# Joints between the six blocks of a two-model transformer kernel: last two output units tile by tile, norm weights at the eviction, constants multiplied meanwhile

## What is computed

```python
h = rmsnorm(x, g[0])
x = x + 0.5 * rmsnorm(swiglu(h, w_gate[0], w_up[0], w_down[0]), g[1])
h = rmsnorm(x, g[2])
x = x + rmsnorm(token_mixer(h, w_in, w_out, ...), g[3])
h = rmsnorm(x, g[4])
x = x + 0.5 * rmsnorm(swiglu(h, w_gate[1], w_up[1], w_down[1]), g[5])
# swiglu: (silu(h @ w_gate) * (h @ w_up)) @ w_down;  256 tokens, width 1024, w_gate and w_up 1024 x 2816
```

## Time and profile before

| what | value |
|---|---|
| median of three runs | 1611.62 us (1608.76 to 1612.12) |
| the profiled execution | 1613.51 us |
| its span in the trace | 1611.7 us |
| PE busy / DVE busy / ACT busy | 92% / 60% / 44% of the span |
| chain that ended last | PE 80%, DVE 8%, ACT 5%, DMA 4% |
| mean granted clock of PE | 0.964 |
| second model begins (last matmul of the first ends) | 514.4 us |

### The profile page before, as it was taken

The page is one execution under the profiler, slowest core; times in us unless marked ns, Lnnn a source line. Parts: engine busy times, 40 slices in busy tenths (PEclk is TensorE's granted clock), DMA queues, the critical chain, the costliest instruction groups (busy, mean ns, idle before and its releaser), DMA issues.

```text
span 1611.7 us, 21802 instructions
## 1 busy us (share of the span) xinstructions
PE 1477.5 (92%) x7995; PEld 1195.7 (74%) x7995; DVE 967.3 (60%) x1508; ACT 709.3 (44%) x1205; POOL 65.1 (4%) x92
## 2 busy tenths in 40 slices
PE   4598999989997999989987999989999899889998
PEld 2476765777853888879866888878888787678886
DVE  1369615344523667676666767776777656576775
ACT  2332215332134444455557444454444555654443
POOL 2000111010001000000000000000000000100000
PEclk9699999999999899999999999989999999999999
DMA  9422138423314565645323565636566443246562
GB/s 321 139 79 79 52 105 282 153 78 114 112 53 148 185 220 171 212 156 183 105 79 118 192 199 183 206 109 223 168 209 206 144 131 110 68 141 229 164 205 74
DMA packets 187807, 246.02 MB, mean 153 GB/s; under 512 B 4224, under 2 KB 168480, under 8 KB 187488
## 3 DMA queue, kind: packets, MB, share of 16 engines
q1 hardware_dynamic: 183872, 229.43, 44.0%
q0 software_dynamic: 3296, 13.64, 2.4%
q10 hardware_dynamic: 576, 2.10, 0.4%
HBM read 244.10 MB, written 1.05 MB: 152 GB/s over the span
## 4 chain that ended last, share of the span: by engine, by line
PE 80%; DVE 8%; ACT 5%; DMA 4%; issue 2%; POOL 1%; SPq 0%; DVEq 0%; ACTq 0%; POOLq 0%
PE bank L1495 30%; PE bank L1919 20%; PE bank L1920 10%; PE bank L1581 4%; DMA weight_ring<-in_w_ada 3%; DVE arena L1220 1%; PE bank L1848 1%; PE bank L1478 1%; PE bank L1899 1%; PE bank L1793 1%; DMA weight_ring<-in_w_ffn_up 1%; DVE weights_low L1226 1%; ACT weights_high L819 1%; PE bank L1516 1%; ACT silu_gate L853 1%
## 5 line engine op out<-in xcount | busy, mean ns | idle before, releaser
L1919 PE MATMUL bank<-input_split,weights_high 128*128 128x512 f32 x1408 | 504.3, 400 | 4.7 <-DVE input_split L1264 4.7
L1226 DVE TENSOR_TENSOR weights_low<-weight_ring,weights_high 128x1024 fp32r<-128x1024 f32 x328 | 396.5, 1224 | 155.6 <-ACT weights_high L819 154.3
L819 ACT ACTIVATE weights_high<-weight_ring 128x1024 fp32r<-128x1024 f32 x328 | 339.5, 1055 | 213.6 <-PE bank L1920 77.7
L1920 PE MATMUL bank<-input_split,weights_low 128*128 128x256 f32 x1408 | 396.8, 282 | 0.0
L1919 PEld LDWEIGHTS bank<-input_split,weights_high 128*128 128x128 f32 x1408 | 266.5, 189 | 71.0 <-issue 6.0
L1920 PEld LDWEIGHTS bank<-input_split,weights_low 128*128 128x128 f32 x1408 | 267.8, 190 | 3.1
L1495 PE MATMUL bank<-weights_high,hidden_high 128*128 128x512 f32 x352 | 138.3, 393 | 0.8 <-DVE hidden_low L1306 0.7
L1495 PE MATMUL bank<-weights_low,hidden_high 128*128 128x512 f32 x352 | 137.9, 392 | 0.0
L1495 PE MATMUL bank<-weights_high,hidden_low 128*128 128x512 f32 x352 | 137.0, 389 | 0.0
L874 ACT ACTIVATE hidden_high<-hidden 128x256 fp32r<-128x256 f32 x88 | 36.8, 418 | 197.9 <-DVE hidden L1302 193.6
L1495 PE MATMUL bank<-input_split,weights_high 128*128 128x256 f32 x512 | 95.7, 288 | 0.7 <-DVE input_split L1264 0.7
(11 more groups left out here) (305 smaller groups left out, 2073.7 us busy)
## 6 DMA issues: line engine op xcount, KB each, us to landing
weight_ring<-in_w_ffn_gate SPq DMA_DIRECT2D x44, 1024.0 KB, 5.9
weight_ring<-in_w_ffn_up SPq DMA_DIRECT2D x44, 1024.0 KB, 5.5
weight_ring<-in_w_ffn_down SPq DMA_DIRECT2D x44, 1024.0 KB, 5.0
weight_ring<-in_w_in SPq DMA_DIRECT2D x42, 1024.0 KB, 5.3
weight_ring<-in_w_ada SPq DMA_DIRECT2D x24, 1024.0 KB, 7.2
weight_ring<-in_w_out SPq DMA_DIRECT2D x16, 1024.0 KB, 4.9
scaled_out<-in_norm_gains POOLq DMA_DIRECT2D x6, 512.0 KB, 3.9
gain_row<-in_norm_gains POOLq DMA_DIRECT2D x6, 512.0 KB, 3.9
```

Of the source, the lines that this page charges most:

```text
L819: A(unit_in(WH, U), unit_source(U), ACT.Copy).then_inc(s_high, 1)
L1226: TTn(unit_in(WL, U), unit_source(U), unit_in(WH, U).bitcast(F32), ALU.subtract).then_inc(s_low, 1)
L1919: mm(b[:, :].rearrange("p (h n) -> p h n", h=2), unit_in(WH, U)[:, k, :], HX[:, k, :, :], start=(k == 0), stop=False, skip_group_check=True)
L1920: last = mm(b[:, 0:T], unit_in(WL, U)[:, k, :], HH[:, k, :], start=False, stop=(k == KD - 1), skip_group_check=True)
```

## The change

- **Output units.** In the last pair of an FFN the second half of the previous down slot is used after both `gate_up`, as unit a+4 (before: a+2). The last two units, both halves of the last down slot, run tile by tile: token tile 0 for both units, then token tile 1. The last two units of a mixer likewise.
- **Tail.** DVE gains and updates token tile 0, then token tile 1.
- **Norm weights.** For the four chunks 0 to 3 (columns 0 to 511) DVE no longer multiplies with `pre_row` (`TS` instead of `STT`); the weight is a per-partition scalar, taken from six added rows of `k_vec2`, and goes in where the transposed chunk is copied out (ACT `scale=`, DVE `STT`). These four chunks are split one by one (128x256), in banks 4 and 5, with waits that keep ACT and DVE in different banks; chunks 4 to 7 in pairs as before. `pre_row` is loaded by half. The transposes of a site now use banks 4, 5, 2, 3.
- **Constants multiplied.** PE starts each `site_norm` with float32 matmuls of the identity with 512 columns of constants into bank 0, four per joint (`WARM`), twelve at site 0. Their result is not used.
- **Splitting ahead.** `EARLY = 2` units of the next site are split before the tail instead of three, so four (`range(EARLY, SPLIT)`) follow after `site_norm`. In a mixer the last two output units are split earlier. The load of the table for the square root moves ahead of the last `hidden_high` of an FFN.

```diff
+EARLY = 2
+WARM = 4
@@ UNITS2
-    UNITS2 += [(m, 0, "c"), (m + 1, 0, "c")] + ([(m - 1, 1, "r")] if q else []) + [(m, 1, "c"), (m + 1, 1, "c"), (m + 2, 0, "r")]
+    back = [(m - 1, 1, "r")] if q else []
+    late = q == FFN_PAIRS - 1
+    UNITS2 += [(m, 0, "c"), (m + 1, 0, "c")] + ([] if late else back) + [(m, 1, "c"), (m + 1, 1, "c")] + (back if late else []) + [(m + 2, 0, "r")]
@@ sync, ffn
-                with sp.Fori(0, FFN_PAIRS - 1) as j:
+                with sp.Fori(0, FFN_PAIRS - 2) as j:
...
+                for q, src in enumerate((g, u, d)):
+                    fill(b0 + 3 * (FFN_PAIRS - 1) + q, src[FFN_PAIRS - 1], 0 if q == 2 else 256)
@@ scalar, site_norm
-                for b in range(4):
-                    act.wait_ge(*at("x_T", "site", i, b))
-                    A(HH[:, 2 * b:2 * b + 2, :], B[b][:, :].rearrange("p (q n) -> p q n", q=2), ACT.Copy).then_inc(*done("input_high", i, b))
+                for c in range(4):
+                    act.wait_ge(*(at("x_T", "site", i, c) if c < 2 else at("input_ready", i, c - 2)))
+                    A(HH[:, c, :], B[4 + c % 2][:, c // 2 * T:(c // 2 + 1) * T], ACT.Copy, scale=vT[:, 2, R_PRE + 8 * i + c:R_PRE + 8 * i + c + 1]).then_inc(*done("input_high", i, c))
+                for c in (4, 6):
...
@@ scalar, ffn, after the loops
+                a, f = a + 5 + 6 * (FFN_PAIRS - 2), f0 + FFN_CHUNKS - 2
+                high(a + 6)
+                silu(0, f + 1, f - 1)
+                hidden_high(0, f + 1, a - 1)
+                for U in range(a + 7, min(len(UNITS2), a + 7 + EARLY)):
+                    high(U)
+                silu(1, f + 2, f)
                 A(stat[:, 60:61], eps[:, 0:1], ACT.Sqrt)
+                hidden_high(1, f + 2, a + 4)
@@ scalar, sites (vector likewise, with low)
-                for unit in range(3, SPLIT):
+                for unit in range(EARLY, SPLIT):
                     high(unit_base[i] + unit)
@@ vector, site_norm
-                    for hf in range(2):
-                        cut = slice(hf * 512, (hf + 1) * 512)
-                        STT(XN2[:, t, cut], X[:, t, cut], stat[:, 12 + t:13 + t], pre_row[:, cut], ALU.mult, ALU.mult).then_inc(*done("x_scaled", "site", i, t, hf))
+                    cut = slice(512, D)
+                    STT(XN2[:, t, cut], X[:, t, cut], stat[:, 12 + t:13 + t], pre_row[:, cut], ALU.mult, ALU.mult).then_inc(*done("x_scaled", "site", i, t, 1))
...
@@ vector, site_tail
-                gained(0, 0)
-                gained(0, 1)
-                gained(1, 0)
-                update(0)
-                gained(1, 1)
-                update(1)
+                for t in range(2):
+                    gained(t, 0)
+                    gained(t, 1)
+                    update(t)
@@ vector, ffn, after the loops
+                gate_sum(0, a + 1)
+                low(a + 6)
+                product(0, a + 2, f + 1)
+                hidden_low(0, f + 1)
+                gate_sum(1, a + 3)
+                for U in range(a + 7, min(len(UNITS2), a + 7 + EARLY)):
+                    low(U)
+                product(1, a + 4, f + 2)
+                hidden_low(1, f + 2)
@@ tensor, site_norm
+                for _ in range(WARM if i else 3 * WARM):
+                    mm(B[0][:, :], ident, KB[:, 0:512], start=True, stop=True)
                 for t in range(2):
...
+                    for c in (0, 2, 1, 3, 4, 5, 6, 7):
@@ tensor, ffn, after the loops
+                gate_up(0, a, f - 1)
+                gate_up(1, a + 2, f)
+                down(1, a + 4, f, False)
+                for t in range(2):
+                    for par in range(2):
+                        pe.wait_ge(s_hl, f + 1 + par)
+                        pe.wait_ge(s_low, a + 6 + par)
+                        last = down_row(par, a + 5 + par, t, False, par == 1)
@@ tensor, mix
-                for k in range(5, KD):
-                    out_rows(k)
+                out_rows(5)
+                for t in range(2):
+                    out_rows(6, (t,))
+                    out_rows(7, (t,))
```

More of the change, by code:

```diff
@@ L824, in _ @@
             act.wait_ge(*at("attn", 1, 0, 1))
-            for unit in range(3):
+            for unit in range(EARLY):
                 high(unit)
@@ L887, in pair @@
                 def pair(a, f, j=None):
-                    split = [U for U in range(a + 6, a + 12) if U < min(len(UNITS2), unit_base[i + 1] + 3)]
+                    split = list(range(a + 6, a + 12))
                     for U in split[0:1]:
@@ L1436, in mix @@
                     split_out(5 + b, B[SB_OUT[b]][:, 0:T], "o_ready")
-                for U in range(u0 + 24, u0 + 29):
-                    low(U + SPLIT)
+                    if b:
+                        low(u0 + 31 + b)
             for i, (kind, n) in enumerate(SITES):
                 site_norm(i)
-                for unit in range(3, SPLIT):
+                for unit in range(EARLY, SPLIT):
                     low(unit_base[i] + unit)
@@ L1936, in gate_up, with down_row, down @@
                         wide_product(B[2 * par + q], U + q, site if q == 0 else None).then_inc(s_used, 1)
-                def down(par, U, ready, first, final, j=None):
+                def down_row(par, U, t, first, final):
+                    for hf in range(2):
+                        last = three(B[4 + 2 * t + hf][:, :], lambda x: HB[x][:, par, t * P:(t + 1) * P], lambda y: W[y][:, U % SPLIT, hf * 512:(hf + 1) * 512], first, final)
+                        if final and (t, hf) != (1, 1):
+                            last.then_inc(*done("y_ready", "site", i, t, hf))
+                    return last
+                def down(par, U, ready, first, j=None):
                     pe.wait_ge(s_hl, ready)
@@ L1941, in down @@
                     for t in range(2):
-                        for hf in range(2):
-                            last = three(B[4 + 2 * t + hf][:, :], lambda x: HB[x][:, par, t * P:(t + 1) * P], lambda y: W[y][:, U % SPLIT, hf * 512:(hf + 1) * 512], first, final)
-                            if final and (t, hf) != (1, 1):
-                                last.then_inc(*done("y_ready", "site", i, t, hf))
+                        last = down_row(par, U, t, first, False)
                     last.then_inc(s_used, 1)
@@ L2132 @@
     rows = [_np.concatenate([a["diff_subln_gain_2"][m]] * 2)[None] for m in range(2)]
-    rows.append(_np.zeros((128 - 2, 128), _np.float32))
+    rows += [a["norm_gains_2"][l, 2 * q].reshape(-1, 128) for l in range(2) for q in range(3)]
+    rows.append(_np.zeros((128 - 50, 128), _np.float32))
     arrays["k_vec2"] = _np.concatenate(rows)
```

96 lines of the change are left out of this document (58 added, 38 removed).

## The result

The changed kernel takes 1633.72 us (median of 4, 1632.49 to 1636.83) where the kernel before took 1611.87 beside it (4, 1608.76 to 1613.05): ratio 1.0142 [1.0121, 1.0162], slower. The profiled execution is 1632.73 with a span of 1630.9, against 1613.51 and 1611.7 before: +19.2 in the two traces.

What follows compares the result with a forecast made beforehand. PE, nearly always at work between joints, was taken as the bound, with FFN-start weights arriving just in time. Site terms summed to 6.1, plus 9.0 for the clock: +15.1, forecast 1626.7 us, range 1614 to 1637.

Steps and rivals of the forecast that it cites:

- Tail and norm: Joint from mixer to FFN: first eviction of the transposed input 2.0 earlier, 1.2 from the tail, 0.8 from scaling and transposes.
- Slots sent for at E + 4.9 and 6.05: FFN start: pair 1's gate and up slots sent for 4.9 and 6.05 after the first eviction of the transposed input.
- Fixed work behind the landing: FFN start: from the up slot's landing to the first down product, split unit 6, multiply, split hidden chunk: 4.35.
- Transfer 7.35: FFN start: the up slot's transfer, 1.15 behind another, takes 7.35; alone it took 5.3.
- PE ready at E + 12.65: FFN start: PE by its own work reaches the first down product 12.65 after the first eviction of the transposed input.
- Clock behind it: After the first-down wait in four FFNs: half clock costs 1.6 to 2.9, taken as 2.25 each, 9.0 in all.
- Second hidden chunk: Last pair of an FFN: the late last down slot makes PE wait 1.9 for the second hidden chunk.
- rival (2): Clock also falls in the 1.9 waits of the last pairs or stays low longer, transfers take 7.8: 1636, chance 0.15.
- Site 1: Mixer: lambdas stand behind the splits, PE waits for a bank, third projection starts 1.2 later; site loses 1.2.
- Site 4: Mixer at site 4: gains 0.2, entered in the sum as -0.2.
- Constants cost nothing: Joints: four constants cost 3.6, twelve 10.6, inside stops of 5.77 and 10.13, so costed at nothing.
- Loop cover of about 6: Further on in the FFN loop: load chain late by 3 to 4, about 6 to spare before a down, costed at nothing.

Runs made afterwards that it cites:

- a_best: Changed kernel with the back unit at its old place, four units split ahead of an FFN, lambdas behind site 1's second projection: 1597.93 us, ratio 0.9904.
- a_fill: Changed kernel plus five float32 constant products (ten records) on PE before each FFN's first down product: 1624.12 us, ratio 1.0074.
- b_early2: Kernel before with only the early splitting changed, two units split ahead instead of three: 1628.51 us, ratio 1.0107.
- s_rows: Changed kernel with the three mends (back unit, four units ahead, lambdas), but the last two output units in the old order: 1599.40 us, ratio 0.9920.
- a_warm4: Changed kernel with four constants instead of twelve ahead of site 0's transposes: 1628.66 us, ratio 1.0099.
- a_early3: Changed kernel with three units instead of two split ahead wherever an FFN follows: 1612.38 us, ratio 0.9999.

## Why the prediction came out as it did

Forecast 1626.7 in 1614 to 1637, slower with 0.84; measured 1633.72. The mechanism was the one forecast: waits before the first downs, released by the load chain, and half clock behind them. The forecast is 7.0 too low. 4.1 of it is in the traces; the rest is mostly that the profiled execution before lay 1.6 over its median and the one after 1.0 under. The sizes, step by step (+19.2 in the traces for +15.1):

- *Tail and norm*: E 2.0 earlier. Measured 1.91 (8.59 to 6.68), at every joint, counted from the last output. First product 0.95 behind E: 1.14. The `TS` was taken 0.3 quicker than the `STT`: 0.49 and 0.75.
- *Slots sent for at E + 4.9 and 6.05*: 5.27 and 6.24 in site 2. *Fixed work behind the landing* 4.35: 894.05 - 889.52 = 4.53.
- *Transfer 7.35*: 7.3, 8.6, 8.4, 7.3. This term was too small, by 1.3 and 1.1 in sites 2 and 3. First down at E + 17.75: 18.1, 19.4, 19.2, 18.1. PE ready at E + 12.65: 13.15 by a_best, 0.5 too early, which hides part of the late landing in the wait. Wait 5.1: 4.79, 6.12, 5.91, 4.80.
- *Clock behind it* 2.25 each, 9.0: half of PE's 4.09, 4.04, 3.75 and 5.27 at 0.50 is 8.6, and a_fill got 7.3 back there. The choice between 0 and 2.9, made by the length of the wait next to 5.77, held four times, but length is not what decides: in b_early2 waits of 2.73 to 3.88 had half clock behind them too, though shorter. The 3.27 to 5.75 for which the clock stays down came from two joints; at the one before site 3 in the kernel before it was at 0.50 from 1066.3 to 1076.5, 9.0 past the first transpose.
- *Second hidden chunk* 1.9: 1.55, 2.33, 1.48. That the clock would not fall there failed once, in site 2, where the wait was longest: 3.41 at half, 1.7 lost. That is a part of rival (2).
- *Site 1* +1.2: 1.67 longer behind the first product, which came 0.33 sooner: 1.3. The bank wait of 1.76 is in the trace, but the sum alone would prove little (next).
- *Site 4* -0.2: measured +0.7. From E to the last output this mixer takes 141.4 before, 141.3 in a_best, 140.3 in s_rows and 143.2 in b_early2, so it wanders by more than the term; in b_early2 two stretches of 3.41 at 0.50 lie in it, in s_rows and before one.
- *Constants cost nothing*: failed at site 0, where they hold the transposes up by 2.7 and E by about 1.5 (12.0 against 10.5 in a_warm4). The prediction compared twelve of them (10.6) with the whole old stop (10.13), but the change also makes the scaled half come sooner, and a filler has to fit the new stop. It cost little in the sum because the load chain set D there.
- *Loop cover of about 6*: held, no waits inside the loops; the seven waits of down products shown above make up the 27.0.
- *Low end of the range*: by the sum's own terms, 9.0 and four times 1.15 off 1626.7, it is 1613.1 and not 1614.

By cuts of the trace, after less before: up to D of site 0 -1.0 (the first model alone -1.5, which no step names), to E of site 1 +1.9, mixer 1 +1.3, to D of site 2 +3.6, to E of site 3 +4.2, to its D +3.7, to E of site 4 +1.6, mixer 4 +0.7, to D of site 5 +2.3, to its last output +2.6, the end -1.7: 19.2. Site 2 with the joint behind it is 3.7 over its forecast (1.3 landing, 1.7 clock behind the second hidden chunk, the rest smaller). The total is only 4.1 short because the others nearly cancel: sites 3, 4 and 5 are 2.7 over, site 0 and the end 2.4 under, of which 1.5 is the first model, where the prediction had nothing. That part of the agreement is luck.

The rule that I weighed, to start a transfer early and wait late (the Trainium skill, "DMA: Bandwidth & Descriptors", section "Rules for kernel authors"), bears on more than the prediction gave it: b_early2 goes against it by one unit for each gate slot and loses 1.1%. The page "TensorE: Matmul & The Clock Gate", section "HAM oscillation — how this bites in real kernels", of the Trainium skill tells of a kernel whose products wait some 3 to 5 us for a transfer at each step and start again at the lower clock every time. The rows agree at all four first downs (4.79 to 6.12), and a_fill got 7.3 back behind them.

Not settled: where the 5.1 between the medians of after and a_warm4 come from, since the second model of the profiled a_warm4, the slowest of its kernel, is only 1.0 shorter; what moves the first model's end by up to 6; how the gain of a_best is shared among its three edits, of which only the early splits were run alone, in the kernel before; and what makes the clock fall behind some waits of 2 us and not behind others.

## What to carry to other kernels

Before moving a split or a copy that frees a buffer, follow the chain from that buffer to the first consumer of what is loaded into it: here one unit split later, so that its slot was sent for 15 us later (865.07 to 879.89), made most of the loss (three quarters when put into the kernel before, all but 0.5 when taken out of the changed one). Speeding up a joint pays only as far as the next thing PE waits for; look which one that is before counting the gain. A filler that keeps the clock up is sized by the stop that remains after the change, and is worth something only where PE, not a load, sets what follows.

## What the runs showed of the hardware that I had not expected

A 1 MB transfer queued 0.97 us behind another took 7.0 to 7.6 where the first took 5.1 to 5.6, and up to 8.7 with one instruction packet (0.02 MB) beside it. Ten records of constants in a wait of 4.8 to 6.1 us kept the granted clock at 1.00 for the work behind it, of which without them 3.75 to 5.27 us ran at 0.50. Waits of 1.48 and 1.55 left the clock up; one of 2.33 in the same place of the code was followed by 3.41 at 0.50. Length alone does not sort them: in a_early3 a wait of 2.48 (D of site 0) left the clock up and one of 1.84 (D of site 5) did not.
